# A decoder block with a 32-expert layer: the residual's columns regrouped for the expert gathers, and the 4 MB weight loads shared between SyncE's queue and ScalarE's

## The chip, the cores and the metric

The kernel runs on one core of one Trainium2 chip. The metric is the device time of one execution in microseconds. Before the change three executions took 1137.30, 1136.61 and 1138.66 us: median 1137.3.

## What is computed

One decoder block on x (256 tokens, 1024 columns, float32). Two branches, block-sparse attention and a gated linear recurrence, are mixed and added to x; then comes a mixture of experts.

```
x = x + mixed @ w_out                        # the residual
h2 = rmsnorm(x, norm2_w)
logits = h2 @ router_w + router_b            # 32 experts, the top 4 of each token, softmax over the 4
for each expert e, for its tokens:
    gu = h2 @ w_gate_up[e] + b_gate_up[e]    # 1024 x 2048, gate and up columns interleaved
    y = ((clip(up) + 1) * gate * sigmoid(1.702 gate)) @ w_down[e] + b_down[e]   # 1024 x 1024
out = rmsnorm(x + sum of weight * y, final_norm_w)
```

All experts' weights are read once: 32 x (8.39 + 4.19) MB = 402.7 MB of the 438 MB that the kernel reads.

## The kernel before, in words

**Front (to about 214 us).** TensorE computes the projections in split precision, both branches, the mixing and `w_out`. Fifteen loads (`LOADS`, L456 to L478) go through a ring of three buffers. GpSimd clears buffers and does the rotary embedding (L556 to L582); its last operation, the clearing at L582, ran at 93.65 us, and nothing follows it. VectorE adds the residual in four pieces (`residual`, L1133), tokens 0 to 127 (tt = 0) and 128 to 255 (tt = 1) by two halves of 512 columns, in place in X; ScalarE sums their squares (`squares`, L780); TensorE transposes them for the router (`turned_x1`, L1641) and forms the logits; VectorE picks the four experts and writes each chosen token's place (`chosen`, `first_places`).

**Experts.** They are done in 16 pairs, with room for 64 tokens each. TensorE first gathers a pair's tokens: `gather` (L1707) multiplies eight blocks of 128 hidden columns (the stationary operand, `hidden`, L1667) by a 0/1 selector of 128 columns, over both token halves: 16 matmuls, each of which the trace shows as two records, so 32. Block k takes every fourth column of a 512-column half, a step of 16 bytes, because the gate-up weights are stored with four neighbouring rows in one partition (`wgu`, L402). The first pair's gather is written out in two halves (`first_gather`, L1670). Per pair then: gate_up of the first expert (L1756), `combine` of the pair before, transposes, gate_up of the second, down of the first (L1808), the gather for the next pair, down of the second. VectorE and ScalarE do the activations in between (`activate`, L1231; `expert`, L816; `drain_y`, L822). `add_residual` (L1837) adds X into the sums once, in pair 12.

**Weights.** They stand in a ring of 11 slots of 2.097 MB in W. A pair needs 12 slots: 0 to 3 and 4 to 7 the gate-up weights of its two experts, 8, 9 and 10, 11 the down weights. "Slot 8 of pair 14" below is m = 8 for j = 14; its place in the ring is (12 j + m) mod 11 (`ring`, L410). Two neighbouring slots are loaded by one transfer of 4 MB (a unit, L454), except where they do not lie side by side (ring place 9), in the first pair, at the start of the second and from slot 4 of the last (`by_slots`, L416): these go slot by slot (L450), the very last in smaller parts (L532). SyncE begins all of them in slot order (`load_pair`, L502), each after it has waited until TensorE has used up what stood in the place before (`used`, L493): slot m of pair j takes the place of slot m + 1 of pair j - 1 (and slot 11 that of slot 0 of the same pair).

```
def used(p, m):
    if m >= 8 and m % 2: sp.wait_ge(y_filled, ...)
    elif m % 4 == 3: sp.wait_ge(gu_filled, ...)
    else: sp.wait_ge(weights_used, ...)
```

ScalarE runs the pairs in a hardware loop (L842) and begins no weight load; its program for a pair is: two sigmoids of the first expert, the copy of selT, two sigmoids of the second, two copies of y, two more copies of y.

Of the kernel before, what the change touches and what calls it, by code (L numbers as in the profile page):

```python
# [125 lines left out]
def hybrid_block(nc, A, out):  # L126
    ctx = ExitStack()
    with ctx:
# [7 lines left out]
        with ExitStack() as early:  # L136
# [20 lines left out]
            over("skip_b2", 1, F32)  # L157
# [115 lines left out]
        n1w, n2c = COLS[:, 0:8], COLS[:, 20:28]  # L273
# [78 lines left out]
        first_sel_ready = sem("first_sel_ready")  # L352
# [86 lines left out]

        block = ctx.enter_context(nc.Block())  # L440
# [3 lines left out]
        def _(sp):  # L444
# [7 lines left out]
            def load_unit(e, j, m):  # L452

                sp.dma_start(slots(ring(j, m), 2), unit_src(e, m)).then_inc(slot_loaded[m], 16)  # L454

            for n, what in enumerate(LOADS):  # L456
# [36 lines left out]
            def used(p, m):  # L493

                if m >= 8 and m % 2:
                    sp.wait_ge(y_filled, p * 2 + (m - 8) // 2 + 1)
                elif m % 4 == 3:
                    sp.wait_ge(gu_filled, (p * 2 + m // 4) * 2 + 2)
                else:
                    sp.wait_ge(weights_used, p * 8 + (m - m // 4 if m < 8 else 6 + (m - 8) // 2) + 1)  # L500

            def load_pair(p, e, j, first_round, stop=12):  # L502

                for m in range(0, stop, 2):
                    if by_slots(j, m, first_round):
                        for n in (m, m + 1):
                            used(p + (n - SLOTS) // 12, (n - SLOTS) % 12)
                            load(e, j, n)
                    else:
                        for n in (m, m + 1):  # L510
                            used(p + (n - SLOTS) // 12, (n - SLOTS) % 12)
                        load_unit(e, j, m)


            for part, done in ((0, half_loaded), (1, slot_loaded[11])):
                if part == 0:
                    sp.wait_ge(half_used, 1)
                else:
                    used(0, 0)
# [9 lines left out]
            for m, c0, c1, done in parts:  # L529
                if c0 == 0:  # L530
                    used(last + (m - SLOTS) // 12, (m - SLOTS) % 12)
# [4 lines left out]
            with sp.If(most > CAP):  # L536
                with sp.Fori(1, ROUNDS) as r:
                    with sp.If(most > r * CAP):
                        for m in range(12):
                            if m < SLOTS:  # L540
                                n = (6 * E - 1 - m) // SLOTS * SLOTS + m
                                used(r * PAIRS + (n // 12 - PAIRS), n % 12)
                            else:
                                used(r * PAIRS, m - SLOTS)
# [38 lines left out]


        @block.scalar
        def _(se):
            st = Steps(se, act_step)
            for r0, n, name in ((0, 8, "norm1_w"), (8, 8, "hgrn_lb_logits"), (16, 4, "hgrn_norm_w"), (20, 8, "norm2_w")):
# [154 lines left out]
            for dst, src in ((RW, A["router_w"].rearrange("l (k p) e -> p (l k) e", p=P)),  # L743
# [98 lines left out]
            with se.Fori(0, E // 2 - 1) as p:  # L842
                pair(p)
# [34 lines left out]
        def _(ve):  # L878
# [17 lines left out]
            drain("rows", v.tensor_copy(COLS[:, 0:28], bank("rows")[:, 0:28]))  # L896
# [289 lines left out]
            st.did(v.tensor_tensor(RW, RW, n2c.unsqueeze(2).to_broadcast([P, KD, E]), ALU.mult), router_ready)  # L1186
# [150 lines left out]
        def _(pe):  # L1337
# [36 lines left out]
            pe.wait_ge(small_loaded, 64)  # L1374
            end(tr(begin("rows")[:, 0:28], ROWS[0:28, :], ident[0:28, 0:28]))
# [265 lines left out]
            def turned_x1(tt, half):  # L1641
# [25 lines left out]
            def hidden(tt, k):  # L1667
                return X[:, tt, 512 * (k // 4) + k % 4:512 * (k // 4) + 512:4]
# [290 lines left out]
```

## Time and profile before

| | us |
|---|---|
| runs | 1136.61, 1137.30, 1138.66 |
| the profiled execution's own time | 1138.16 |
| its span | 1136.4 |
| PE busy | 1110.3 (98%) |
| PE weight loads busy | 566.8 (50%) |
| VectorE, ScalarE, GpSimd busy | 349.2, 224.3, 38.9 |
| mean granted TensorE clock | 0.998 |
| DMA, mean over the span | 387 GB/s |

The span runs from the first to the last instruction; the execution takes 1.8 us more. Matmuls are pipelined, so two records overlap: the pitch between starts says what one costs, not its duration. The DMA share is the mean busy share of the 16 DMA engines. A chain piece is the time that one group of instructions held up the end.

### The profile page before, as it was taken

What the parts mean: (1) busy time and instruction counts of PE and PEld (TensorE: products, weight loads), DVE (VectorE), ACT (ScalarE), POOL (GpSimd) and SP (SyncE); (2) the same over time, 40 slices, a digit from 0 to 9 for tenths busy, and PEclk for the clock granted to TensorE, in tenths of its full rate; (3) what the DMA queues carried; (4) which work ended last, traced back from release to release, by engine and by line L of the source; (5) the groups of instructions that cost most, each with busy time, mean ns of one, the idle gap of its engine ahead of it and who ended that gap; (6) DMA issues with size and microseconds to landing.
All of it is one profiled execution on the core that took longest, in us unless ns stands there. A gap on an engine that the chain in (4) does not pass through costs nothing.

```text
span 1136.4 us, 12828 instructions
## 1 busy us (share of the span) xinstructions
PE 1110.3 (98%) x5341; PEld 566.8 (50%) x5341; DVE 349.2 (31%) x691; ACT 224.3 (20%) x357; POOL 38.9 (3%) x32
## 2 busy tenths in 40 slices
PE   7999999999999999999999999999999998999997
PEld 7889888735353535353535353535353534353532
DVE  4983887332222221213130303030303031222113
ACT  7645774121010101010101010101010101010102
POOL 0380000000000000000000000000000000000000
PEclk9999999999999999999999999999999999999999
DMA  9545479999999999999999999999999999999995
GB/s 315 194 149 213 157 253 364 363 411 393 405 429 432 431 433 428 432 431 430 431 432 430 431 432 426 434 434 427 427 436 426 438 427 427 435 427 428 430 424 211
DMA packets 36478, 439.64 MB, mean 387 GB/s; under 512 B 3980, under 2 KB 6440, under 8 KB 21320
## 3 DMA queue, kind: packets, MB, share of 16 engines
q1 hardware_dynamic: 34192, 436.71, 92.0%
q10 hardware_dynamic: 2232, 2.13, 0.6%
q8 instruction: 44, 0.72, 0.3%
q14 instruction: 10, 0.08, 0.0%
HBM read 437.78 MB, written 1.05 MB: 386 GB/s over the span
## 4 chain that ended last, share of the span: by engine, by line
PE 83%; DMA 14%; DVE 1%; issue 0%; ACTq 0%; ACT 0%; DVEq 0%; SPq 0%
PE PS L1763 30%; PE PS L1821 18%; DMA W<-in_w_down_dram 14%; PE PS L1713 10%; PE PS L1733 4%; PE PS L1420 3%; PE PS L1424 3%; PE PS L1427 3%; PE PS L1406 3%; PE PS L1783 1%; PE PS L1803 1%; PE PS L1386 1%; PE PS L1673 1%; PE PS L1459 1%; DMA ROWS<-in_norm_w_dram 0%
## 5 line engine op out<-in xcount | busy, mean ns | idle before, releaser
L1763 PE MATMUL PS<-W,M 128*64 128x512 f32 x2048 | 456.0, 597 | 5.8 <-issue 2.9
L1763 PEld LDWEIGHTS PS<-W,M 128*64 128x64 f32 x2048 | 142.7, 137 | 288.8 <-issue 279.9
L1821 PE MATMUL PS<-W,M 128*64 128x512 f32 x1024 | 226.4, 594 | 5.9 <-DMA W<-in_w_down_dram 5.9
L1236 DVE TENSOR_SCALAR M<-PS 128x256 f32<-128x256 f32 x64 | 27.0, 423 | 494.9 <-PE PS L1763 494.9
L1821 PEld LDWEIGHTS PS<-W,M 128*64 128x64 f32 x1024 | 73.0, 137 | 145.2 <-issue 139.9
L820 ACT ACTIVATE M<-M 128x256 f32<-128x256 f32 x64 | 26.6, 416 | 458.5 <-DVE M L1236 458.5
L1713 PE MATMUL PS<-M,X 128*128 128x128 f32 x480 | 114.4, 397 | 0.0
L1713 PEld LDWEIGHTS PS<-M,X 128*128 128x128 f32 x480 | 113.1, 329 | 0.0
L825 ACT COPY M<-PS 64x512 f32<-64x512 f32 x31 | 17.9, 578 | 312.6 <-PE PS L1821 312.6
L1733 PE MATMUL PS<-M,SELT 128*128 128x512 f32 x120 | 55.5, 605 | 0.0
L1250 DVE COPY M<-PS 128x512 f32<-128x512 f32 x32 | 22.1, 692 | 108.5 <-PE PS L1803 108.5
L1227 DVE TENSOR_TENSOR M<-PS,SMALL 128x512 f32<-128x512 f32 x32 | 22.1, 692 | 91.4 <-PE PS L1713 88.2
L1244 DVE TENSOR_TENSOR M<-M 128x256 f32<-128x256 f32 x64 | 38.9, 608 | 2.2
L1733 PEld LDWEIGHTS PS<-M,SELT 128*128 128x128 f32 x120 | 21.6, 189 | 33.7 <-issue 33.7
L437 DVE TENSOR_TENSOR w_lo<-W,hi_a 128x2048 fp32r<-128x2048 f32 (+1 forms) x16 | 32.5, 2055 | 13.4 <-ACT hi_a L621 13.4
L1424 PE MATMUL PS<-w_lo,hT_hi 128*128 128x512 f32 x128 | 31.6, 389 | 0.0
L1240 DVE SCALAR_TENSOR_TENSOR M<-M 128x256 f32<-128x256 f32 x64 | 27.2, 425 | 2.2
L621 ACT CAST hi_a<-W 128x2048 fp32r<-128x2048 f32 (+1 forms) x16 | 26.6, 1695 | 1.6 <-DMA W<-in_w_in_dram 1.6
L1424 PEld LDWEIGHTS PS<-w_lo,hT_hi 128*128 128x128 f32 x128 | 24.0, 188 | 5.1
L1238 DVE TENSOR_SCALAR M<-PS 128x256 f32<-128x256 f32 x64 | 26.5, 414 | 0.0
L1783 PE MATMUL PS<-bias_parts,pick 128*128 128x512 f32 x64 | 23.4, 447 | 0.0
L1783 PEld LDWEIGHTS PS<-bias_parts,pick 128*128 128x128 f32 x64 | 9.5, 188 | 26.0 <-issue 26.0
(258 smaller groups left out, 814.1 us busy)
## 6 DMA issues: line engine op xcount, KB each, us to landing
W<-in_w_gate_up_dram SPq DMA_DIRECT2D x51, 4096.0 KB, 35.6
W<-in_w_down_dram SPq DMA_DIRECT2D x25, 4096.0 KB, 32.4
W<-in_w_gate_up_dram SPq DMA_DIRECT2D x26, 2048.0 KB, 21.8
W<-in_w_down_dram SPq DMA_DIRECT2D x11, 2048.0 KB, 40.7
W<-in_w_in_dram SPq DMA_DIRECT2D x10, 2048.0 KB, 8.0
W<-in_w_down_dram SPq DMA_DIRECT2D x5, 1024.0 KB, 41.3
W<-in_w_out_dram SPq DMA_DIRECT2D x2, 2048.0 KB, 10.5
W<-in_w_in_dram SPq DMA_DIRECT2D x2, 1024.0 KB, 9.2
```

Of the source, the lines that this page charges most:

```text
L437: tensor_tensor(raw_part(what, j, lo=True), raw_part(what, j), hi_part(PIECES[n][3]), ALU.subtract).then_inc(lo_ready[PIECES[n][2]], 1)
L1240: v.scalar_tensor_tensor(out=up[:, c], in0=up[:, c], scalar=1.0, in1=gate[:, c], op0=ALU.add, op1=ALU.mult).then_inc(up_ready, 1)
L1244: v.tensor_tensor(act.rearrange("p (c q) -> p q c", c=4)[:, 64 * half:64 * half + 64, :], up[:, c].rearrange("p (q c) -> p q c", c=4), sg[ ...
L1406: ins = mm(ps[:, T * a:T * a + T], w[:, k, P * a:P * a + P], x[:, k, :], start=(k == 0 and w is w_h and x is hT_hi), stop=(k == KD - 1 and ...
L1420: mm(ps[:].rearrange("p (j n) -> p j n", j=2), hi[:, k, rows], w_h[:, k, 2 * half:2 * half + 2], start=(k == 0), stop=False)
L1424: mm(ps[:], hi[:, k, rows], w_l[:, k], start=False, stop=False)
L1427: ins = mm(ps[:].rearrange("p (j n) -> p j n", j=2), lo[:, k, rows], w_h[:, k, 2 * half:2 * half + 2], start=False, stop=(k == kn - 1))
L1713: ins = mm(dst[:, P * a:P * a + P], hidden(tt, 4 * part + a), sel[:, tt, :], start=(tt == 0), stop=(tt == TT - 1))
L1733: mm(acc[tt][n][:], selT[:, P * tt:P * tt + P], Y[:, 512 * n:512 * n + 512], start=False, stop=True, skip_group_check=True)
L1763: ins = mm(gate_rows(half, g), hTe[:, k, tok], cols[:, :, g, :], start=(k == 0), stop=(k == KD - 1))
L1783: mm(gu[half][:], pick[:, b].rearrange("p g s -> p (g s)"), bias_parts[:, 512 * half:512 * half + 512], start=False, stop=False, skip_grou ...
L1821: ins = mm(dst[64 * n:64 * n + 64, :], actT[b][:, k, 64 * kh:64 * kh + 64], dn_slot[slot][:, k, 512 * n:512 * n + 512], start=(kh == 0 and ...
```

## The change

The residual is kept in another column order. While the front still runs, GpSimd copies x so that within each 512-column half the columns 4q + k stand at 128k + q; the two token halves also change places in X, with a spare page (`x_spare`, in W's slot 9 of the first pair, which is why SyncE waits for the copies before that load). The gathers then read 128 neighbouring columns. The residual addition and `add_residual` read or write with a step of 128 columns instead; the router's weights and `norm2_w` are laid out to match. Of the units, those with m = 2, 6 and 10 are begun by ScalarE, in its own queue, at three places of its program for a pair, whose loop is written out for the first 15 pairs; SyncE begins the rest as before.

```diff
--- before.py
+++ after.py
-            over("skip_b2", 1, F32)
+            x_spare = over("x_spare", 1, F32)
...
+        def rows_of(tt):
+            return X[:, 1 - tt, :]
+        def half_rows(tt, half):
+            return rows_of(tt)[:, 512 * half:512 * half + 512].rearrange("p (k q) -> p q k", k=4)
...
+        def by_scalar(j, m, first_round):
+            return m % 4 == 2 and not by_slots(j, m, first_round)
+        def load_unit(eng, e, j, m):
+            for n in (m, m + 1):
+                used(eng, j + (n - SLOTS) // 12, (n - SLOTS) % 12)
+            eng.dma_start(slots(ring(j, m), 2), unit_src(e, m)).then_inc(slot_loaded[m], 16)
...
                 if what == "wo1":
+                    sp.wait_ge(x_regrouped, 1)
                     load(0, 0, 9)
...
                 for m in range(0, stop, 2):
                     if by_slots(j, m, first_round):
                         for n in (m, m + 1):
-                            used(p + (n - SLOTS) // 12, (n - SLOTS) % 12)
+                            used(sp, p + (n - SLOTS) // 12, (n - SLOTS) % 12)
                             load(e, j, n)
-                    else:
-                        for n in (m, m + 1):
-                            used(p + (n - SLOTS) // 12, (n - SLOTS) % 12)
-                        load_unit(e, j, m)
+                    elif not by_scalar(j, m, first_round):
+                        load_unit(sp, e, j, m)
...
+            def regroup(to, x):
+                for half in range(2):
+                    c = slice(512 * half, 512 * half + 512)
+                    ins = nc.gpsimd.tensor_copy(to[:, c].rearrange("p (k q) -> p q k", k=4),
+                                                x[:, c].rearrange("p (q k) -> p q k", k=4))
+                return ins
+            pool.wait_ge(at_ready, 1)
+            pool.wait_ge(xn_ready, TT)
+            st.did(regroup(x_spare, X[:, 0, :]))
+            st.settle()
+            st.did(regroup(rows_of(1), X[:, 1, :]))
+            st.settle()
+            nc.gpsimd.tensor_copy(rows_of(0), x_spare).then_inc(x_regrouped, 1)
...
-            for dst, src in ((RW, A["router_w"].rearrange("l (k p) e -> p (l k) e", p=P)),
+            for dst, src in ((RW.rearrange("p (u k) e -> p u k e", k=4), A["router_w"].rearrange("l (u p k) e -> p (l u) k e", p=P, k=4)),
...
-                st.did(nc.scalar.activation(squares_junk, X[:, tt, c], ACT.Square, accum_out=ssp[:, tt, n:n + 1]))
+                st.did(nc.scalar.activation(squares_junk, rows_of(tt)[:, c], ACT.Square, accum_out=ssp[:, tt, n:n + 1]))
...
-            def pair(p, last=False):
+            def begin_unit(j, m):
+                if j < PAIRS and by_scalar(j, m, True):
+                    load_unit(se, 2 * j, j, m)
+            def pair(p, last=False, loads=False):
                 expert(p * 2, 0)
+                if loads:
+                    begin_unit(p, 10)
                 se.wait_ge(selT_filled, p + 1)
                 nc.scalar.copy(selT, gath[:, 0:T]).then_inc(selT_drained, 1)
                 expert(p * 2 + 1, 1)
+                if loads:
+                    begin_unit(p + 1, 2)
                 drain_y(p * 2, 0)
+                if loads:
+                    begin_unit(p + 1, 6)
...
-            with se.Fori(0, E // 2 - 1) as p:
-                pair(p)
+            for p in range(PAIRS - 1):
+                pair(p, loads=True)
...
-                xs = X[:, tt, 512 * n:512 * n + 512]
-                drain(name, v.tensor_tensor(xs, bank(name)[:], xs, ALU.add))
+                xs = half_rows(tt, n)
+                drain(name, v.tensor_tensor(xs, bank(name)[:].rearrange("p (q k) -> p q k", k=4), xs, ALU.add))
...
-            st.did(v.tensor_tensor(RW, RW, n2c.unsqueeze(2).to_broadcast([P, KD, E]), ALU.mult), router_ready)
+            ve.wait_ge(n2w_loaded, 16)
+            st.did(v.tensor_tensor(RW, RW, n2w.unsqueeze(2).to_broadcast([P, KD, E]), ALU.mult), router_ready)
+            ve.wait_ge(x_regrouped, 1)
             residual(0, 0)
...
-                    ins = tr(ps[:, P * a:P * a + P], X[:, tt, c:c + P], ident)
+                    ins = tr(ps[:, P * a:P * a + P], rows_of(tt)[:, c:c + P], ident)
...
             def hidden(tt, k):
-                return X[:, tt, 512 * (k // 4) + k % 4:512 * (k // 4) + 512:4]
+                return rows_of(tt)[:, P * k:P * k + P]
...
-                        mm(acc[tt][n][:], ident, X[:, tt, 512 * n:512 * n + 512], start=False, stop=True,
+                        mm(acc[tt][n][:].rearrange("p (q k) -> p q k", k=4), ident, half_rows(tt, n), start=False, stop=True,
                            skip_group_check=True)
```

Left out: the semaphore's declaration, `used` moved out of SyncE's program with the engine as an argument and its other calls, and the norm2_w rows, which are no longer loaded into ROWS and COLS (28 columns become 20).

## Rows read from the trace of the kernel before

**Rows 1.** The page's GB/s in 40 equal slices of the span.
```profile
GB/s 315 194 149 213 157 253 364 363 411 393 405 429 432 431 433 428 432 431 430 431 432 430 431 432 426 434 434 427 427 436 426 438 427 427 435 427 428 430 424 211
```

**Rows 2.** Busy time by stretch: PE, PEld, DVE, ACT, POOL, PEclk, DMA share, GB/s.
```profile
225.00:300.00 75.00, 73.25 (x319) 29.58 (x316) 19.96 (x55) 12.04 (x21) 0.00 (x0) 1.00 0.97 397
300.00:780.00 480.00, 480.00 (x2133) 210.13 (x2133) 99.92 (x247) 47.49 (x85) 0.00 (x0) 1.00 1.00 430
780.00:1080.00 300.00, 291.41 (x1272) 125.46 (x1270) 57.86 (x145) 29.37 (x52) 0.00 (x0) 0.99 1.00 431
```

**Rows 3.** Chain by time, pair 0 to 1 (start us, us, what).
```profile
268.25 7.46 PE PS L1713 x32
...
282.74 10.30 PE PS L1763 x48
...
297.28 3.63 PE PS L1733 x8
...
301.63 10.45 PE PS L1763 x48
...
316.33 6.87 PE PS L1821 x32
...
323.78 7.46 PE PS L1713 x32
```

**Rows 4.** The same chain, late.
```profile
779.18 39.32 DMA W<-in_w_down_dram
...
1121.83 3.68 PE PS L1821 x16
```

**Rows 5.** The gather's group on the page, and contiguous ones in the chain.
```profile
L1713 PE MATMUL PS<-M,X 128*128 128x128 f32 x480 | 114.4, 397 | 0.0
...
10.84 7.88 PE PS L1386 x64
...
207.52 1.71 PE PS L1655 x16
```

**Rows 6.** The first gather's second half in the chain; VectorE's bias parts in its timeline.
```profile
219.55 4.00 PE PS L1673 x16
...
229.90 2.61 DVE L1276 TENSOR_TENSOR bias_parts<-M,bias_parts 32x512 fp32r<-32x512 f32 x4 [5.42 <-ACT bias_parts L807]
```

**Rows 7.** SyncE's issues in its timeline (start us, us, what).
```profile
162.48 0.58 SPq L450 DMA_DIRECT2D W<-in_w_down_dram  x1
...
254.41 0.33 SPq L454 DMA_DIRECT2D W<-in_w_gate_up_dram  x1
...
264.32 0.33 SPq L454 DMA_DIRECT2D W<-in_w_gate_up_dram  x1
...
293.12 0.33 SPq L454 DMA_DIRECT2D W<-in_w_gate_up_dram  x1
```

**Rows 8.** ScalarE's timeline: first y copy of pair 0, second sigmoid of pair 1.
```profile
267.71 0.58 ACT L825 COPY M<-PS 64x512 f32<-64x512 f32 x1 [7.19 <-PE PS L1821]
...
299.52 0.42 ACT L820 ACTIVATE M<-M 128x256 f32<-128x256 f32 x1 [3.04 <-DVE M L1236]
```

**Rows 9.** An idle gap late in the chain, what followed, and the stretch's clock.
```profile
958.33 2.89 issue
961.23 12.16 PE PS L1763 x48
...
960.00:965.00 5.00, 3.77 (x10) 1.29 (x12) 0.00 (x0) 0.85 (x1) 0.00 (x0) 0.66 1.02 436
```

**Rows 10.** Groups: residual additions, GpSimd's nearest operation; GpSimd's timeline: its last operation.
```profile
L1137 DVE TENSOR_TENSOR X<-PS,X 128x512 f32<-128x512 f32 x4 | 2.7, 686 | 5.2 <-PE PS L1637 5.2
...
L579 POOL TENSOR_TENSOR W<-W 128x256 f32<-128x256 f32 x4 | 4.8, 1205 | 0.0
...
93.65 0.52 POOL L582 MEMSET W<- 64x512 f32 x1 [11.36 <-ACT W L692]
```

**Rows 11.** The page's DMA issues: KB each, median us to landing.
```profile
W<-in_w_gate_up_dram SPq DMA_DIRECT2D x51, 4096.0 KB, 35.6
```

More of the change, by code:

```diff
@@ L271, in h3 @@
             return ap.rearrange("p (h t) -> p h t", h=GH)
-        n1w, n2c = COLS[:, 0:8], COLS[:, 20:28]
+        def rows_of(tt):
+            return X[:, 1 - tt, :]
+        def half_rows(tt, half):
+            return rows_of(tt)[:, 512 * half:512 * half + 512].rearrange("p (k q) -> p q k", k=4)
+        n1w = COLS[:, 0:8]
         lbrow0, lbrow1, hnw = COLS[:, 8:12], COLS[:, 12:16], COLS[:, 16:20]
@@ L351, in hybrid_block @@
         root2_ready, rstd2_ready, xn2_ready = sem("root2_ready"), sem("rstd2_ready"), sem("xn2_ready")
-        first_sel_ready = sem("first_sel_ready")
+        first_sel_ready, x_regrouped = sem("first_sel_ready"), sem("x_regrouped")
         lgmax_ready, lgexp_ready, mask_ready, wts_ready, rounds_ready = (
@@ L438, in form_lo, with used @@
                           ALU.subtract).then_inc(lo_ready[PIECES[n][2]], 1)
+        def used(eng, p, m):
+            if m >= 8 and m % 2:
+                eng.wait_ge(y_filled, p * 2 + (m - 8) // 2 + 1)
+            elif m % 4 == 3:
+                eng.wait_ge(gu_filled, (p * 2 + m // 4) * 2 + 2)
+            else:
+                eng.wait_ge(weights_used, p * 8 + (m - m // 4 if m < 8 else 6 + (m - 8) // 2) + 1)
+        def by_scalar(j, m, first_round):
[4 more added lines that the diff above has]
+            eng.dma_start(slots(ring(j, m), 2), unit_src(e, m)).then_inc(slot_loaded[m], 16)
         block = ctx.enter_context(nc.Block())
@@ L450, in load @@
                 sp.dma_start(slots(ring(j, m)), slot_src(e, m)).then_inc(slot_loaded[m], 16)
-            def load_unit(e, j, m):
-                sp.dma_start(slots(ring(j, m), 2), unit_src(e, m)).then_inc(slot_loaded[m], 16)
             for n, what in enumerate(LOADS):
@@ L491, in _ @@
                 load(0, 0, m)
[L493 to L498, printed above, removed]
-                else:
-                    sp.wait_ge(weights_used, p * 8 + (m - m // 4 if m < 8 else 6 + (m - 8) // 2) + 1)
             def load_pair(p, e, j, first_round, stop=12):
@@ L506, in load_pair @@
                         for n in (m, m + 1):
-                            used(p + (n - SLOTS) // 12, (n - SLOTS) % 12)
+                            used(sp, p + (n - SLOTS) // 12, (n - SLOTS) % 12)
                             load(e, j, n)
-                    else:
-                        for n in (m, m + 1):
-                            used(p + (n - SLOTS) // 12, (n - SLOTS) % 12)
-                        load_unit(e, j, m)
+                    elif not by_scalar(j, m, first_round):
+                        load_unit(sp, e, j, m)
             for part, done in ((0, half_loaded), (1, slot_loaded[11])):
@@ L518, in _ @@
                 else:
-                    used(0, 0)
+                    used(sp, 0, 0)
                 sp.dma_start(slots(ring(0, 11))[:, 2048 * part:2048 * part + 2048],
@@ L530, in _ @@
                 if c0 == 0:
-                    used(last + (m - SLOTS) // 12, (m - SLOTS) % 12)
+                    used(sp, last + (m - SLOTS) // 12, (m - SLOTS) % 12)
                 sp.dma_start(slots(ring(last, m))[:, 1024 * c0:1024 * c1],
@@ L541, in _ @@
                                 n = (6 * E - 1 - m) // SLOTS * SLOTS + m
-                                used(r * PAIRS + (n // 12 - PAIRS), n % 12)
+                                used(sp, r * PAIRS + (n // 12 - PAIRS), n % 12)
                             else:
-                                used(r * PAIRS, m - SLOTS)
+                                used(sp, r * PAIRS, m - SLOTS)
                             load(0, 0, m)
@@ L587, in _ @@
             st = Steps(se, act_step)
-            for r0, n, name in ((0, 8, "norm1_w"), (8, 8, "hgrn_lb_logits"), (16, 4, "hgrn_norm_w"), (20, 8, "norm2_w")):
+            for r0, n, name in ((0, 8, "norm1_w"), (8, 8, "hgrn_lb_logits"), (16, 4, "hgrn_norm_w")):
                 se.dma_start(ROWS[r0:r0 + n, :], A[name].rearrange("a (r c) -> (a r) c", c=P)).then_inc(small_loaded, 16)
@@ L895, in _ @@
             filled(ve, "rows")
-            drain("rows", v.tensor_copy(COLS[:, 0:28], bank("rows")[:, 0:28]))
+            drain("rows", v.tensor_copy(COLS[:, 0:20], bank("rows")[:, 0:20]))
             st.settle()
@@ L1373, in _ @@
             pe.wait_ge(ident_loaded, 16)
-            pe.wait_ge(small_loaded, 64)
-            end(tr(begin("rows")[:, 0:28], ROWS[0:28, :], ident[0:28, 0:28]))
+            pe.wait_ge(small_loaded, 48)
+            end(tr(begin("rows")[:, 0:20], ROWS[0:20, :], ident[0:20, 0:20]))
             for tt in range(TT):
```

## The prediction

> **What bounds the kernel now.** I read the busy table by stage first [rows 1, 2]. After 300 us TensorE looks full (480.00 of 480 us) but so is the transfer path: share 1.00 at 430 GB/s until 780, and 1.00 at 431 afterwards, where TensorE first falls short (291.41 of 300). The chain by time says which of the two gives way. One pair of experts takes TensorE from gather to gather 323.78 - 268.25 = 55.53 us [rows 3]. A pair's weights are 12 slots of 2.097 MB = 25.17 MB, which at 430 GB/s is 58.5 us. So TensorE asks for 3 us a pair more than arrives, lives on the 11 slots loaded ahead, and has used them up by about 780: from there the chain runs through transfers [rows 4], and it ends 1121.8 us in, when the last slot has landed, plus 14.6 us of finish. **The transfer stream bounds the kernel**, although TensorE shows 98%. What can still be won lies in the stream's idle time: 225 to 300 us has share 0.97 [rows 2], that is 75 x 0.03 = 2.3 us, and nothing after.
>
> The profiled execution took 1138.2 us (span 1136.4 and 1.8 around it), 0.9 above the median of 1137.3. The sum is made against 1138.2 and 0.9 is taken off at its end.
>
> **Part one: the gathers.** Hidden columns are read with a step of four elements today; 32 records take 7.46 us, a pitch of 233 ns (397 ns each, overlapped) [rows 3, 5]. Contiguous 128x128 float32 stationaries have a pitch of 1.71/16 = 107 ns (32 moving columns) and 7.88/64 = 123 ns (128 moving columns, as here) [rows 5]. I take 110: a gather falls from 7.46 to 3.5 us, 4.0 us each, 15 times: 60 us less of TensorE work. Its price on the path is almost nothing, because the stream needs 58.5 us a pair whether TensorE needs 55.5 or 51.5; TensorE only starts to wait for weights earlier: the lead that lasted 480 us at 3 us a pair (25 us) lasts 3.5 pairs at 7 us. What counts is the opening. The first gather (two halves, the second 4.00 us at 219.55 [rows 6]) ends 4 us earlier, so the first slots are released at 219.5 instead of 223.55. But TensorE then reaches the bias matmuls 10.45 us later [rows 3], at 230.0, and VectorE finishes the bias parts at 232.5 [rows 6]: 1.5 us earlier than today's 234.0 is all that passes. The gather at 268 adds 4. These fill the idle 2.3 us of the stream before 300. Bounds: 0 (the opening is held by bias and routing work instead) to -3; taken: **-2.3**.
>
> The same regrouping adds to the front: GpSimd copies 2 x 1024 columns by halves, strided, plus 1024 straight. Its nearest row is 1205 ns for 256 columns [rows 10]: 2.4 us per half, 4 halves and two more for the straight copy = 14 us, at double price 29. It starts when its last clearing is done, at 94.2 us [rows 10], and ends by 108 to 123; SyncE waits for it only ahead of slot 9's first load, at 162.48 us [rows 7], and VectorE only ahead of the residual, later still. Hidden by 39 us at least; gone, each us of it would hold back `w_out`'s second load by one. The four residual additions (686 ns each [rows 10]) now read and write with a step of 128 elements. No row has that step on VectorE; the far bound is the factor that the strided weight load shows, 233/107 = 2.2, which is +0.8 us each; the other is 0. Two of the four stand on the way to the routing, while TensorE has w_out work beside the others: 0 to +1.6, taken **+0.3** (TensorE has other work beside most of it). The `add_residual` matmuls (4, once) read their moving side with that step: up to 2.2 times their time, some 4 us, in pair 12, where TensorE then has 58.5 - 51.5 = 7 us to spare: 0. The narrower `rows` transpose, one DMA less and the router load in longer pieces lie in the front, beside TensorE's work: 0.
>
> **Part two: units over two queues.** Now SyncE issues in slot order, each as soon as its slots are free. Units with m = 2, 6, 10 go to ScalarE's program, which reaches them only after its own work: m = 10 after both sigmoids of a pair's first expert, m = 2 after those of the second, m = 6 after the copies of y. An issue costs 0.33 us of ScalarE, three a pair, and the waits there are already satisfied when it arrives; behind it stand copies with 4 us of gather beside them: 0. The lateness is what costs.
>
> While the queue is deep (35.6 us from issue to landing [rows 11]) 10 us later does no harm. In the first pairs it isn't deep. The unit issued at 254.41 ends its 4.19 MB 9.75 us later, at 264.2, and the next is issued at 264.32 [rows 7]: no reserve. That one is m = 6 of pair 1; ScalarE can begin it only behind its y copies, at 267.71 + 0.6 [rows 8], while slot 8 of the same pair, for which SyncE waits until that same y is there, comes first, at 267.7: the stream idles 267.7 - 264.2 = **+3.5 us** (all of it 1.5 us earlier in the new kernel, hence the same gap). Then m = 10 of pair 1, which ScalarE reaches only after the second sigmoid, 299.5 today [rows 8], while SyncE begins the unit after it at 293.12 [rows 7]. In the new kernel the stream restarts at 267.7 - 1.5 = 266.2 with slot 8, unit 6 and slot 9, 8.39 MB = 19.5 us, and is empty at 285.7; SyncE's next unit goes out at 293.1 - 5.5 = 287.6: **+1.9**. Later the queue deepens by itself. Bounds 0 to +8 (0 if the earlier slots leave reserve).
>
> The order of landing is the other term. Two queues that share the stream give each half, so a unit that is needed second can land beside or before one that is needed first. Where the queues alternate, that only uses up lead. Near the end there is none: in pair 14, slots 6 and 7 (ring place 9, loaded singly) go by SyncE, so slots 4 to 8 all stand in SyncE's queue while ScalarE's brings slot 10. If all came in order, 14 slots (10 and 11 of pair 14, 12 of pair 15) would follow the unit at slot 8: 29.4 MB = 68.3 us, plus 3.7 of TensorE after the last [rows 4] = 72.0. TensorE's own work from there is, from rows 3 with the short gather, 7.0 + 0.6 + 3.5 + 7.0, then 14.5 + 4.35 + 14.7, then 7.0 + 0.6 + 7.0 = 66.3 us. Spare: 5.7. One unit ahead of its turn delays slot 8 by up to 9.75 us: up to +4.1 beyond the stream's end, 0 at the other end; taken the middle, **+2**.
>
> Rate: no row has the two queues busy at once. 430 GB/s at share 1.00 in one queue speaks for no gain; I take 0, with bounds of one per cent either way (the full slices of rows 1 read 424 to 438): 820 us x 0.01 = 8.2 us.
> The Trainium skill, "DMA: Bandwidth & Descriptors", section "Issuing engines are not separate dma queues", says that DMAs begun by different engines run on the same 16 DMA engines and interleave, so that spreading them saves issue time alone; by it the rate term is 0. Its specifications give a ceiling of 435 GB/s; an estimate from that page would be a gain of at most 1.2%.
>
> Sum: 1138.2 - 2.3 + 0.3 + 3.5 + 1.9 + 2 = 1143.6; less 0.9, **1143**.
>
> **Rivals.** A. *The second queue raises the rate.* If one queue leaves a short hole at each packet, two fill it: one per cent gives 1143 - 8 = 1135. For: share 1.00 counts packets' time, not bytes. Against: 430 whether units or single slots are queued. It decides from 0.7% on (5.7 of 820 us). Faster.
> B. *Lateness costs nothing.* The earlier slot releases leave a reserve and landing order evens out: only part one is left, 1137.3 - 2.3 = 1135.
> C. *TensorE loses its clock.* It now waits 7 us a pair, in pieces that the order of landing sets. A gap of 2.89 us at 958 was followed by 48 records in 12.16 us, against 10.45 [rows 9, 3], at a granted 0.66 over the next 5 us, so partly at the 1.2 GHz level: 1.7 us for each such gap. In the middle the 7 spare us swallow it; in the last 66 us there is no spare, so two gaps are +3.4: 1147. Or interleaved streams read worse by 1%: 1150.
> The Trainium skill, "TensorE: Matmul & The Clock Gate", section "Part 1: The HAM clock gate", says that the throttled clock is the default and that activity releases it; the trace's gap of 2.89 us agrees.
> D. *The gather stays at 7.46 us* (the step was not its cause). Then the late issues stand without the earlier slots: 1137.3 + 5.4 + 4.1 = 1147.
>
> **Chances.** Forecast 0.45 (its own range 1139 to 1148), A 0.20, B 0.15, C 0.15, D 0.05. Faster by over 0.2% (2.3 us, about what a measurement of this kernel can tell from no change): A and half of B, a few of the forecast's low end: 0.30. Within: rest of B and the forecast's low end: 0.14. Slower 0.56. The range takes the rate gain with the shorter idle, 1131, to C's 1149.
>
> **What would show it.** Right: L1713's group near 110 ns pitch; stream share below 0.95 between 255 and 300 us, then 1.00 at 430; TensorE waiting for weights from about 500 us on, 7 us a pair, longest near 1055; ScalarE's issues at 0.33 us. Wrong: a rate of 433 or more from 300 on (A); no idle before 300 (B); granted clock under 1.00 in the last 70 us (C); gathers still 7.5 us (D).

## The result, and the profile after

The changed kernel takes **1146.0 us** (median of five runs, 1144.0 to 1151.9) against 1137.3 (median of five, 1136.6 to 1138.7) for the kernel before on the same chip: a ratio of 1.0079, 95% interval 1.0062 to 1.0095. It is slower by 8.7 us. The profiled execution was the quickest of its five, 1144.0 us with a span of 1142.2; against the 1138.2 of the profile before, its trace has 5.8 us to account for, not the whole 8.7.

The page's groups for the gather, the two large products and the residual addition, then its queues and the median times from issue to landing:

```profile
q1 hardware_dynamic: 28720, 277.32, 58.9%
q10 hardware_dynamic: 6920, 161.51, 33.0%
...
L1809 PE MATMUL PS<-W,M 128*64 128x512 f32 x2048 | 467.4, 608 | 32.3 <-DMA W<-in_w_gate_up_dram 23.5
...
L1867 PE MATMUL PS<-W,M 128*64 128x512 f32 x1024 | 234.6, 612 | 20.5 <-DMA W<-in_w_down_dram 20.5
...
L1759 PE MATMUL PS<-M,X 128*128 128x128 f32 x480 | 56.1, 275 | 0.0
...
W<-in_w_gate_up_dram SPq DMA_DIRECT2D x26, 4096.0 KB, 40.8
W<-in_w_gate_up_dram ACTq DMA_DIRECT2D x25, 4096.0 KB, 26.4
```

The gather did what it was meant to: 480 records, 114.4 us busy before [rows 5] and 56.1 now, 275 ns each in place of 397. TensorE waits for weights instead, 23.5 + 20.5 = 44 us, where the kernel before waited 6.9; three pauses marked "issue" (0.80, 2.59 and 1.14 us) are such waits too: each ends 0.1 us after a unit of weights has landed, as is shown for the last of them below. And the two queues are not alike: a unit in SyncE's queue (q1, 277 MB, against 161.5 in q10) takes 40.8 us from issue to landing, one in ScalarE's 26.4; all took 35.6 before [rows 11].

The windows, columns as in rows 2, with two short ones in the opening:

```profile
225.00:300.00 75.00, 71.36 (x322) 26.57 (x320) 21.55 (x57) 11.12 (x21) 0.00 (x0) 0.98 0.92 375
300.00:780.00 480.00, 447.55 (x2056) 172.57 (x2054) 96.09 (x240) 35.69 (x74) 0.00 (x0) 0.97 1.00 431
780.00:1080.00 300.00, 282.41 (x1302) 111.20 (x1300) 60.16 (x149) 22.94 (x47) 0.00 (x0) 0.98 1.00 430
...
265.00:270.00 5.00, 5.00 (x34) 2.76 (x31) 0.89 (x2) 1.16 (x2) 0.00 (x0) 1.00 0.39 118
285.00:290.00 5.00, 5.00 (x24) 1.59 (x20) 0.00 (x0) 0.00 (x0) 0.00 (x0) 1.00 0.80 338
```

Against rows 2: the rate at full share is 431 and 430, as with one queue. Before 300 us the share has fallen from 0.97 to 0.92, that is 75 x 0.05 = 3.75 us of additional idle time, and the two short windows show two places: 5 x 0.61 = 3.1 us at 265 to 270 and 5 x 0.20 = 1.0 us at 285 to 290. The issues around them, from the timelines of SyncE and ScalarE:

```profile
254.78 0.33 SPq L468 DMA_DIRECT2D W<-in_w_gate_up_dram  x1
...
268.08 0.33 SPq L480 DMA_DIRECT2D W<-in_w_down_dram  x1
...
268.15 0.36 ACTq L468 DMA_DIRECT2D W<-in_w_gate_up_dram  x1
```

A unit goes out at 254.8 and nothing else until 268.1, when SyncE's slot 8 and ScalarE's unit m = 6 start together. The end of the chain by time:

```profile
1020.37 43.17 DMA W<-in_w_down_dram
1063.67 7.09 PE PS L1867 x32
1071.34 3.57 PE PS L1759 x32
1074.92 7.02 PE PS L1867 x32
1081.93 1.14 issue
1083.07 10.52 PE PS L1809 x48
...
1120.84 10.47 PE PS L1867 x48
```

The last transfer in this chain is slot 8 of pair 14, issued at 1020.37 and used at 1063.67. From there TensorE works to the end, 1120.84 + 10.47 = 1131.31, which is 67.6 us with one pause of 1.14 us, ahead of the first slot of pair 15. The profile marks it "issue", because it names no releaser. It is a wait for a transfer all the same. That slot's unit, from SyncE's timeline, and its way from the view of the DMA issues in these microseconds:

```profile
1038.46 0.33 SPq L468 DMA_DIRECT2D W<-in_w_gate_up_dram  x1
...
W<-in_w_gate_up_dram SPq DMA_DIRECT2D x1, 4096.0 KB, 44.5
```

It lands at 1038.46 + 44.5, about 1083.0, and the products start at 1083.07. Nothing after that waits for a transfer, so the last 48.2 us are TensorE's alone. Before, the chain went through a transfer for the last time at 1121.83 and those products ended at 1121.83 + 3.68 = 1125.51 [rows 4]. **The end has passed from the stream to TensorE**, and the two ends differ by 1131.31 - 1125.51 = 5.8 us, which is all of the trace's difference. In the kernel before, slot 8 of pair 14 was used at 1053.45, so it now comes 10.2 us later; from it to the last product took 72.05 us (1125.51 - 1053.45) and takes 67.6, 4.4 less. 10.2 - 4.4 = 5.8. Half of the 10.2 is a later issue (1020.37 against 1015.27: 5.1 us), half a longer way (43.3 from issue to use against 38.2: 5.1).

### The profile page after: what moved, and what is told of

Its sections match the earlier page's. It is cut to its first block, busy times and chain, and to the rows that moved or that the text cites. A ratio compares the mean times of both kernels' runs of the same rounds, so it can differ in the third digit from the quotient of the medians.

```text
span 1142.2 us, 12700 instructions
## 1 busy us (share of the span) xinstructions
PE 1072.6 (94%) x5341; PEld 512.3 (45%) x5341; DVE 351.1 (31%) x691; ACT 206.1 (18%) x343; POOL 44.1 (4%) x37
## 4 chain that ended last, share of the span: by engine, by line
PE 63%; DMA 32%; DVE 2%; issue 1%; another core or an unknown queue 0%; ACT 0%; ACTq 0%; DVEq 0%; SPq 0%
DMA W<-in_w_down_dram 23%; PE PS L1809 21%; PE PS L1867 15%; DMA W<-in_w_gate_up_dram 8%; PE PS L1759 4%; PE PS L1466 3%; PE PS L1470 3%; PE PS L1473 3%; PE PS L1779 3%; PE PS L1452 3%; DMA M<-in_b_gate_up_dram 1%; PE PS L1829 1%; PE PS L1849 1%; PE PS L1432 1%; PE PS L1505 1%
## 5 line engine op out<-in xcount | busy, mean ns | idle before, releaser
L1809 PE MATMUL PS<-W,M 128*64 128x512 f32 x2048 | 467.4, 608 | 32.3 <-DMA W<-in_w_gate_up_dram 23.5
L1809 PEld LDWEIGHTS PS<-W,M 128*64 128x64 f32 x2048 | 147.3, 139 | 323.6 <-issue 289.4
L1867 PE MATMUL PS<-W,M 128*64 128x512 f32 x1024 | 234.6, 612 | 20.5 <-DMA W<-in_w_down_dram 20.5
L1867 PEld LDWEIGHTS PS<-W,M 128*64 128x64 f32 x1024 | 75.7, 141 | 165.6 <-issue 163.8
L857 ACT COPY M<-PS 64x512 f32<-64x512 f32 x31 | 17.9, 578 | 277.9 <-PE PS L1867 277.9
L1759 PE MATMUL PS<-M,X 128*128 128x128 f32 x480 | 56.1, 275 | 0.0
L1759 PEld LDWEIGHTS PS<-M,X 128*128 128x128 f32 x480 | 54.8, 192 | 0.0
## 6 DMA issues: line engine op xcount, KB each, us to landing
W<-in_w_gate_up_dram SPq DMA_DIRECT2D x26, 4096.0 KB, 40.8
W<-in_w_gate_up_dram ACTq DMA_DIRECT2D x25, 4096.0 KB, 26.4
```

The costliest lines, as they stand in the source:

```text
L1759: ins = mm(dst[:, P * a:P * a + P], hidden(tt, 4 * part + a), sel[:, tt, :], start=(tt == 0), stop=(tt == TT - 1))
L1809: ins = mm(gate_rows(half, g), hTe[:, k, tok], cols[:, :, g, :], start=(k == 0), stop=(k == KD - 1))
L1867: ins = mm(dst[64 * n:64 * n + 64, :], actT[b][:, k, 64 * kh:64 * kh + 64], dn_slot[slot][:, k, 512 * n:512 * n + 512], start=(kh == 0 and ...
```

## The experiments

Ratios are against the kernel before, run beside each on the same chip (its medians 1137.5 to 1138.0), with 95% intervals. `by_scalar` decides which units ScalarE begins; it is the line that most of the edits change.

**Gather alone.** All units by SyncE, the rest of the change kept.

```diff
-            return m % 4 == 2 and not by_slots(j, m, first_round)
+            return False
```

> The changed kernel with all units begun by SyncE again; columns stay regrouped and ScalarE's loop stays written out. Theory (late issues in the opening and the order of landing at the end cost the time; the gathers alone gain a little idle of the stream): no gap of several us at 250 to 300 us, stream share there 0.98 or more, end set by the last transfer, 1133 to 1137 us. Rival G (the regrouping itself or the written-out loop costs): 1142 us or more. Rival Q (two queues carry less): 430 GB/s here and in the changed kernel alike would speak against it.

Measured: 1137.9 us (12 runs), ratio 1.0000 (0.9992 to 1.0009). So the whole loss is the second queue's, and nearly sixty microseconds less of TensorE work are worth nothing that can be measured. Part of where the expected 2 us went shows at the end, in the chain and in a window of 4 us (columns as in rows 2):

```profile
1040.98 41.65 DMA W<-in_w_gate_up_dram
1082.67 5.25 PE PS L1809 x16
...
1096.46 10.45 PE PS L1809 x48
...
1115.18 10.47 PE PS L1867 x48
```

```profile
1082.00:1086.00 4.00, 3.33 (x8) 1.00 (x10) 0.00 (x0) 0.00 (x0) 0.00 (x0) 0.57 1.04 440
```

TensorE waited 3.6 us for slot 2 of the last pair; the sixteen matmuls behind the wait took 5.25 us where others like them take 3.65, at a granted clock of 0.57, partly the 1.2 GHz level. From there TensorE has no wait for a transfer left, so these 1.6 us are lost for good. In the opening, see below, little of the earlier release came through.

**Queues alone.** The kernel before with nothing but the division over two queues.

```diff
+        def by_scalar(j, m, first_round):
+            return m % 4 == 2 and not by_slots(j, m, first_round)
...
-                    else:
-                        for n in (m, m + 1):
-                            used(p + (n - SLOTS) // 12, (n - SLOTS) % 12)
-                        load_unit(e, j, m)
+                    elif not by_scalar(j, m, first_round):
+                        load_unit(sp, e, j, m)
```

> The kernel before with only the units divided over two queues; gathers stay at 7.46 us. Theory: without the short gathers the idle before 300 us grows from about 7 to 10 or 12 us, and TensorE, with 70 us of its own work after the unit at slot 8 of pair 14, has 4 us less in hand at the end: 1149 to 1156 us, the slowest of all. Rival (the queues cost a fixed 8 us whatever the gathers take): 1143 to 1147. Rival G: 1137 to 1139.

Measured: 1153.8 us (4 runs), ratio 1.0143 (1.0128 to 1.0158).

```profile
260.00:270.00 10.00, 10.00 (x48) 5.12 (x47) 1.87 (x4) 1.18 (x3) 0.00 (x0) 1.00 0.68 267
280.00:290.00 10.00, 10.00 (x50) 3.37 (x48) 0.00 (x0) 1.16 (x2) 0.00 (x0) 1.00 0.80 342
290.00:300.00 10.00, 10.00 (x38) 3.52 (x35) 4.75 (x16) 0.83 (x2) 0.00 (x0) 1.00 0.67 262
```

The three windows are short of 10 x (0.32 + 0.20 + 0.33) = 8.5 us of stream (4 in the changed kernel by the same reckoning over these windows). Without the shorter gather the second queue costs 16 us, with it 8. TensorE's timeline shows where. Its last wait for a transfer stands ahead of the first slot of pair 11, again marked "issue"; below it are the way of that slot's unit, begun by SyncE at 804.56, and of the unit that ScalarE began at 828.33:

```profile
857.22 12.06 PE L1780 MATMUL PS<-W,M 128*64 128x512 f32 x48 [7.52 <-issue]
...
W<-in_w_gate_up_dram SPq DMA_DIRECT2D x1, 4096.0 KB, 52.6
...
W<-in_w_gate_up_dram ACTq DMA_DIRECT2D x1, 4096.0 KB, 25.0
```

SyncE's unit lands at 804.56 + 52.6, about 857.2, when TensorE's wait ends. ScalarE's unit was begun 24 us later and landed some 4 us earlier, at about 853.3, though it holds slots used after SyncE's. This one wait costs 7.5 us, and the products behind it another 1.6 (12.06 for the 10.45 of rows 3). The 280 us after that, with four gathers of 7.46 us, are TensorE's own, but for a pause of 3.23 us at 973.5 that the profile doesn't explain (the kernel before has one of 2.89 at the same place of the program [rows 9]). There a gather that is 3.9 us shorter counts until the stream is the bound again; in one queue, where the stream is the bound, it counts nothing.

**Opening by SyncE**, and **end by SyncE**: the two suspected places, taken out one at a time, and then both.

```diff
-            return m % 4 == 2 and not by_slots(j, m, first_round)
+            return j >= 3 and m % 4 == 2 and not by_slots(j, m, first_round)
```

> The changed kernel, but ScalarE begins units only from pair 3 on; the opening is SyncE's. Theory: the gaps before 300 us close (share 0.98), the end stays TensorE's: 5 us less than the changed kernel, 1139 to 1143. Rival O (only the order of landing counts, the idle is made up later): no change, 1145 to 1147.

Measured: 1145.0 us (6 runs), ratio 1.0070 (1.0055 to 1.0084). A miss: the gaps are closed, and only 1 us is won. The window, and the end of the chain:

```profile
225.00:300.00 75.00, 71.64 (x330) 26.84 (x328) 21.55 (x57) 11.12 (x21) 0.00 (x0) 1.00 1.01 418
```

```profile
1015.98 45.86 DMA W<-in_w_down_dram
1061.97 8.70 PE PS L1867 x32
...
1119.39 10.47 PE PS L1867 x48
```

Here slot 8 of pair 14 is issued at 1015.98, practically as before (1015.27), and takes 46.0 us to its use in place of 38.2: 7.8 us longer. That is nearly one unit's 9.75 us, with no idle time in the stream to share the blame. The trace shows what went ahead of it: ScalarE begins its unit of pair 14 (m = 10, used after slot 8) at 1038.52, and from then to 1061.9, when slot 8 is used, ScalarE's queue moves 4.39 MB, which is 10.2 us of the stream at 430 GB/s. In one queue none of that would stand ahead of slot 8.

```profile
q10 hardware_dynamic: 149, 4.39, 43.8%
```

```diff
+            return j < 13 and m % 4 == 2 and not by_slots(j, m, first_round)
```

> The changed kernel, but pairs 13 to 15 are loaded by SyncE alone. Theory: the gaps before 300 us stay (share 0.92), TensorE has its spare at the end again and the last transfer ends the run: 1138 to 1142. Rival I (the idle is the whole cost): no change, 1145 to 1147. If TensorE's lower clock after its waits is what costs at the end, granted clock in the last 70 us rises here.

Measured: 1142.0 us (7 runs), ratio 1.0033 (1.0020 to 1.0046). The opening's window, and the chain's last transfer:

```profile
225.00:300.00 75.00, 71.47 (x330) 26.76 (x328) 21.54 (x57) 11.13 (x21) 0.00 (x0) 1.00 0.95 389
```

```profile
1041.98 43.37 DMA W<-in_w_gate_up_dram
1085.39 5.35 PE PS L1809 x16
```

The last wait is again the one for slot 2 of the last pair, as in the gather-alone kernel, 2.7 us later than there (1085.39 against 1082.67), and the stream lacks 0.02 more of its share in the opening than there, 75 x 0.02 = 1.5 us. The end's order is repaired, the opening's idle time stands. The other 1.2 us are not traced to a place.

```diff
+            return 3 <= j < 13 and m % 4 == 2 and not by_slots(j, m, first_round)
```

> The changed kernel, but SyncE begins all units of pairs 0 to 2 and 13 to 15; ScalarE has its share of pairs 3 to 12 only. Theory: both costs are gone, and ten pairs over two queues cost nothing, since the stream is full there either way: 1136.5 to 1139, as with one queue. Rival (sharing the queues costs in every pair): 1141 or more.

Measured: 1136.9 us (11 runs), ratio 0.9991 (0.9982 to 1.0001). Ten pairs of two queues cost nothing. The matmuls on slot 8 of pair 14, from TensorE's timeline, in this kernel and then in the one with only its opening by SyncE:

```profile
1051.12 7.06 PE L1867 MATMUL PS<-W,M 128*64 128x512 f32 x32
```

```profile
1061.97 8.70 PE L1867 MATMUL PS<-W,M 128*64 128x512 f32 x32 [6.71 <-DMA W<-in_w_down_dram]
```

Without ScalarE's share in the last three pairs the slot is there when TensorE comes (1051.12, no wait); with it TensorE waits 6.7 us, loses clock behind the wait (8.70 for 7.09), and starts 10.9 us later. The four kernels as a table (medians; the kernel before had 1137.3 beside the first, 1137.8 beside the next two and 1138.0 beside the last):

| ScalarE's units | opening late | opening by SyncE | the opening costs |
|---|---|---|---|
| also at the end | 1146.0 | 1145.0 | 1.1 |
| not at the end | 1142.0 | 1136.9 | 5.1 |
| the end costs | 4.1 | 8.1 | together 9.1 |

The two costs do not add: the opening costs some 4 us less where the end is late too, give or take 3 by the intervals of the four ratios. So with ScalarE's units in the last pairs, a fuller stream in the opening hardly ends the kernel earlier. How much fuller it is must be read from traces whose opening ran at the same clock: 1.00 against 0.95 of the stream's share with the units of the end by SyncE, 75 x 0.05 = 3.75 us. The 0.92 of the changed kernel's trace has in it that TensorE ran at a granted clock of 0.74 from 235 to 240 us, where the kernel with its opening by SyncE (1.01) had 1.00.

**Lateness or order?** One queue, but SyncE waits, from pair 3 on, for what ScalarE's program would have waited for before those units.

```diff
-                    elif not by_scalar(j, m, first_round):
+                    else:
+                        if first_round and j >= 3 and m % 4 == 2:
+                            if m == 6:
+                                sp.wait_ge(y_filled, 2 * j - 1)
+                            else:
+                                sp.wait_ge(gu_filled, 4 * j + 2 if m == 10 else 4 * j)
                         load_unit(sp, e, j, m)
```

> One queue (SyncE) for all units, but from pair 3 on SyncE holds back the units with m = 2, 6, 10 until the moment at which ScalarE would have begun them. The same units as in the third experiment, equally late, in slot order. If lateness by itself costs at this depth of queue: 1143 or more, like the third experiment (1145). If it is the order of landing that costs: as the first experiment, 1136 to 1139.

Measured: 1139.2 us (12 runs), ratio 1.0012 (1.0002 to 1.0022). The kernel with one queue and no such waits stands at 1.0000, the one with two queues from pair 3 on at 1.0070. So late issues by themselves cost some 1.2 us, no more than the noise, and what remains of the 8.1 us of the table needs the second queue: the order in which the transfers land. The lateness is matched nearly, not wholly: the unit m = 10 of pair 14 goes out 17.9 us behind slot 8 here, 22.5 in the kernel with two queues. Its page shows units that start later and are on their way for 33.8 us, not 42.1 as in the one-queue kernel, and slot 8 used at 1051.63:

```profile
W<-in_w_gate_up_dram SPq DMA_DIRECT2D x51, 4096.0 KB, 33.8
```

```profile
1051.63 8.78 PE L1872 MATMUL PS<-W,M 128*64 128x512 f32 x32 [2.33 <-DMA W<-in_w_down_dram]
```

**The clock behind the last wait.** The gather-alone kernel with four matmuls of 384 columns on a free PSUM bank ahead of slot 2 of the last pair; their results are used by nothing.

```diff
+                    if m == 0 and s == 2 and isinstance(at[0], int) and at[1] == PAIRS - 1:
+                        for _ in range(4):
+                            keep_clock(gath, 384)
```

> The first experiment's kernel with only the filler matmuls of the last pair. Clock theory: 1 to 2 us below the first experiment (1136 to 1137). Rival (the last transfer ends the run): 1138.

Measured: 1136.1 us (12 runs), ratio 0.9982 (0.9974 to 0.9991): 1.9 us quicker than without.

```profile
1078.81 2.85 PE L1664 MATMUL PS<-CST 128*128 128x384 f32 x8
1081.89 3.65 PE L1809 MATMUL PS<-W,M 128*64 128x512 f32 x16 [0.23 <-DMA W<-in_w_gate_up_dram]
```

The fillers take up the wait and the matmuls behind it run in 3.65 us again. The traces of all kernels with units of the last pair by SyncE agree, but for one: without fillers these matmuls took 5.25 to 5.35 us in four, behind waits of 3.0 to 3.6 us, and 3.65 in the late-bias kernel below, behind 3.30; with fillers they took 3.65 in all four.

**The bias wait in the opening.** In the changed kernel TensorE reaches the bias matmuls of the first expert some 2 us before VectorE has the parts. Two ways round it. First, the gather-alone kernel with these matmuls put behind most of slot 3's products, and the same with the filler at the end:

```diff
+                    elif late_bias:
+                        for half in range(2):
+                            one(half, 6, slot, 0)
+                        pe.wait_ge(bias_ready, 4)
+                        for half in range(2):
+                            add_bias(half)
+                            one(half, 7, slot, 1).then_inc(gu_filled, 1)
```

> One queue and short gathers as in the first experiment, and in the first expert the bias matmuls stand in the fourth slot instead of behind the third, so that TensorE isn't stopped by the bias load. Theory (the opening of the short-gather kernel is held by the bias chain, which is why its gathers won nothing before 265 us): the gap of the stream near 250 to 255 us shrinks by 1 to 2 us, time 0.5 to 2 us below the first experiment's. Rival: no change, the bound lies elsewhere.

Measured: 1139.9 us (11 runs), ratio 1.0020 (1.0008 to 1.0031). A miss, and on the wrong side.

> As the one before, and in the last pair four matmuls of 384 columns on a free bank fill TensorE's wait for slot 2 (2.6 us of work, a wait of 3.6). Theory (in the short-gather kernels TensorE's own work of 43 us from there ends the run, and part of it runs at the lower clock): slot 2's matmuls fall from 5.3 to 3.5 us, time 1 to 2 us below the one before: 1133 to 1136. Rival (the last transfer ends the run): no change.

Measured: 1138.2 us (11 runs), ratio 1.0005 (0.9997 to 1.0014). The difference to the one ahead is 1.6 us, as with the filler above. The traces don't show it: in the one without fillers the wait happened to cost no clock. The absolute time missed for the same reason as there.

```profile
235.00:245.00 10.00, 6.00 (x20) 1.63 (x18) 5.83 (x19) 2.12 (x3) 0.00 (x0) 0.71 1.00 403
...
255.00:260.00 5.00, 5.00 (x21) 1.51 (x19) 0.00 (x0) 0.00 (x0) 0.00 (x0) 1.00 0.38 111
```

These windows are of the late-bias kernel. The wait was only moved, TensorE has 6.00 us of work in the ten from 235, and the clock falls to 0.71. The activations depend on the bias as before, the unit after them goes out at 257.12 instead of 255.86, and the stream's share falls to 0.38 at 255 to 260.

Second, fillers in the wait itself: the kernel with the end filler and three more matmuls ahead of the bias wait.

```diff
+                                if m == 0:
+                                    for _ in range(3):
+                                        keep_clock(bank("wT"), 384)
```

> The kernel of the end filler (one queue, short gathers; 1136.1) with three matmuls of 384 columns (1.9 us) in TensorE's wait for the bias parts as well. Theory (the short first gather makes TensorE wait for the bias and lose its clock, and slot 5 is released at 254.8 to 255.9 instead of 254.4 in such runs, 252.9 with full clock): release at 252.5 to 253.7, granted clock 1.00 from 232 to 240, 1 to 2 us below: 1134 to 1135.5. Rival (the opening has no part in it): 1136.

Measured: 1135.8 us (11 runs), ratio 0.9980 (0.9971 to 0.9989). The unit goes out at 253.57 instead of 255.24 and the share of 225 to 300 us rises from 0.98 to 1.00, but the time is the same within 0.2 us. Nor is the earlier issue surely the fillers': four kernels without them (opening, end or both by SyncE, and late issues in one queue) also kept a granted clock of 1.00 there and issued it at 252.9 to 253.7. From slot 2 of the last pair on, the end is TensorE's (its last wait for a transfer ends at 1081.8, as it did at 1081.9 with the end filler alone), and stream time won in the opening does not show in it.

**Both fillers and two queues in the middle.**

> Both fillers, and ScalarE's queue for pairs 3 to 12 only. Theory: the same as with one queue, 1134 to 1135.5, since the middle is bound by the stream at 430 GB/s with one queue or two. Rival (the second queue helps where order can be made up): 1 us or more below the one before.

Measured: 1135.4 us (11 runs), ratio 0.9984 (0.9975 to 0.9994), no different from the one ahead. Its windows, beside rows 2:

```profile
225.00:300.00 75.00, 73.25 (x334) 27.79 (x332) 21.55 (x57) 11.13 (x21) 0.00 (x0) 1.00 1.00 418
300.00:780.00 480.00, 449.41 (x2092) 175.70 (x2090) 98.32 (x244) 36.88 (x76) 0.00 (x0) 0.97 1.00 431
```

The best version found is thus the changed kernel with one queue and the filler at the end, 0.2% (some 2 us) faster than the kernel before; a second queue adds nothing to it.

## Why the prediction was right, and where its terms were not

The forecast was 1143 in a range of 1131 to 1149, slower with 0.56. It came out at 1146.0, slower, by the mechanism of the forecast: late issues in the opening and the order of landing at slot 8 of pair 14. The sizes of the terms were wrong in both directions, and that their sum came so near is in good part luck. Term by term:

- **The bound.** Right. After 300 us the stream's share stays 1.00 at 430 to 431 GB/s in every kernel run, whichever engine begins the units. Rival A (a higher rate) falls with that, and the rule cited there from the Trainium skill, "DMA: Bandwidth & Descriptors", section "Issuing engines are not separate dma queues", agrees: on this core a second issuing queue brought no bandwidth.
- **The gather's size.** Taken as 3.5 us at a pitch of 110 ns; measured 3.57 us (3.57/32 = 111.6 ns). Rival D falls.
- **What the gather is worth, -2.3.** This is the term that failed: measured 0.0 (1.0000, 0.9992 to 1.0009). The prediction said "1.5 us earlier than today's 234.0 is all that passes" in the opening. In the gather-alone trace the bias matmuls do start 1.3 us earlier (232.62 for 233.93), but the unit issued at 254.41 in the kernel before [rows 7] goes out at 255.86, later: TensorE has waited 2.3 us for the bias parts and comes out of the wait with a granted clock of 0.56 over 235 to 240. In four other traces with the short gather, where the wait was 1.2 to 1.8 us and the clock stayed at 1.00, it goes out between 252.9 and 253.7, 0.7 to 1.5 us earlier, as the step had it. The prediction let the gain pass to an end set by the last slot's landing; in this kernel the last wait for a transfer is the one for slot 2 of the last pair, and the 43 us behind it are TensorE's. And at the end 1.6 us go to the clock, of which the filler kernel gives 1.9 back. That these two make up the whole 2.3 is an inference; the filler shows the second directly.
- **The late issues, +3.5 and +1.9.** Places right, size too large as idle time of the stream: 75 x 0.05 = 3.75 us, whether the share falls from 1.00 to 0.95 (opening at full clock) or from 0.97 to 0.92 (behind a lost clock), not 5.4. The net of the opening, 5.4 - 2.3 = 3.1 forecast and 3.75 there, came near only because the gain of 2.3 was missing too. The gaps are 3.1 and 1.0 us at 265 to 270 and 285 to 290. SyncE's unit, then slot 8 and ScalarE's m = 6 together at 268.1, is the order that was forecast, for 266.2. In the time it is worth 5.1 us where the end lets it through.
- **The order of landing, +2 in 0 to 4.1.** The mechanism and its place (slot 8 of pair 14 stands in SyncE's queue while ScalarE's unit, used later, takes part of the stream) are what the traces show; the size was too small. Alone it costs 8.1 us, with the late opening 4.1. By the chain: the prediction had a delay of up to 9.75 and 5.7 to spare, and took half; the delay measured is 10.2 (5.1 of it from the later issue) and the spare 4.4. TensorE takes 67.6 us from slot 8 on, not 66.3, and 1.1 of that is the wait for the first slot of pair 15 at 1081.93, which the prediction didn't have; its sum of TensorE's own work is right.
- **Why the sum held all the same.** The terms were added, and they don't add: the opening costs 5.1 alone and 1.1 on top of the end's. Alone the two places cost 5.1 + 8.1 = 13.2, where 7.4 was taken; that each hid part of the other was not forecast, and is the luck in it. In medians against 1137.8, the kernel whose second queue works only in the middle stands at -0.9, where part one was taken as -2.0; the two places of the second queue together cost 9.1. 1.1 + 1.7 = 2.8 are the 3 us by which the forecast was low.
- **Rival C (clock loss).** Partly there. The clock of 300 to 780 us is 0.97 and of 780 to 1080 0.98 (1.00 and 0.99 before), mostly swallowed by the time to spare there; in the last 66 us it took 1.6 us in the gather-alone kernel, and of the 16 us of the kernel with nothing but the two queues 1.6 stand behind its wait of 7.5. In the profile of the changed kernel slot 8's products ran in 7.09 us after a wait of 2.0, so there it does not explain the loss.
- **Rival B (lateness costs nothing).** Refuted by the share of 0.92 and by the table.
- **The costs put at nothing.** GpSimd's copies take 5.2 us in all, 94.5 to 99.8, not 14 to 29, and are hidden. `add_residual` takes 6.98 us in the chain, 3.44 before, 2.0 times, in pair 12. The size is right; that it is hidden is open: the final chain has no transfer between 888 and 1020 and runs through it, and no kernel was run without its step. The residual additions take 1072 ns for 686 [rows 10], 1.56 times, +0.39 us each, two of them ahead of the routing: +0.8 at most where 0.3 was taken.
- **A sign that was read too loosely.** "7 us a pair from about 500 on": the first wait for weights is at 391, 1.9 us; over 300 to 780 TensorE idles 480 - 447.55 = 32.45 us, 4.0 a pair of 58.5. The rest of the 7 is the lower clock and the lead. The longest waits are of 5.7 and 5.4 us, at 741 and 522, not near 1055; the two that set the end are only 2.0 and 1.1 us long.

## What to carry to other kernels

When a queue is the bound, shortening another engine's work only moves its waits; ask first which idle time of the stream it can fill. A second queue on a saturated stream brings no bandwidth but lets transfers needed later land ahead of those needed first: harmless while several buffers are in reserve, paid where the reserve is gone, so keep the last transfers of such a stream in one queue and in the order of their use. And don't add the costs of two delays before it is clear that the same engine is the bound behind both: here the smaller was nearly hidden by the larger. And where a profile gives no reason for a pause, set its end beside the landings of the transfers: most pauses marked "issue" here were waits for one.

## What the runs showed of the hardware that was not expected

- Units in the less loaded queue pass those in the other: 26.4 us from issue to landing against 40.8, while the rate over both stays 430 GB/s. In the kernel with nothing but the two queues a unit of 4 MB begun 24 us after another landed 4 us ahead of it.
- A wait of TensorE of 2 to 4 us sometimes costs clock and sometimes not. A wait of 3.6 us was followed by a granted clock of 0.57 over 4 us, one of 3.3 us by none; ahead of slot 8 of pair 14 one of 2.34 us was followed by 32 records in 8.8 us (late-bias and end-filler kernels) and one of 2.35 by 7.09 (end by SyncE). In the opening the waits for the bias of 2.0 to 2.3 us cost clock in three traces, those of 1.2 to 1.8 in none of four. Three 384-column matmuls in a pause of 2.8 us there kept it at 1.00; four at the end gave back 1.9 us.
- A float32 operand read with a step costs each engine differently, 128 elements' step against contiguous: TensorE's moving side 6.98 us for 3.44 (2.0 times), VectorE's addition 1072 ns for 686 (1.56 times). GpSimd's copy of 128x512 with a step of 4 elements in what it reads took 1110 to 1128 ns, and its contiguous one of 128x1024 took 1.04 us:

```profile
94.47 2.06 POOL L604 COPY x_spare<-X 128x512 f32<-128x512 f32 x2
96.59 2.10 POOL L604 COPY X<-X 128x512 f32<-128x512 f32 x2
98.75 1.04 POOL L614 COPY X<-x_spare 128x1024 f32<-128x1024 f32 x1
```
